# A finer-stepped opening behind dummy matmuls, and two weight subtractions given to GpSimd at the boundary into latent attention

## The reference, cut to what matters

```python
def dilated_mixer(x, w_in, w_out, cos, sin):
    h = x @ w_in                      # 2048 x 20480, in fp32
    ...
def mla_mixer(x, w_in, ...):
    h = x @ w_in
...
for layer in range(DEPTH):
    ...
    x = layer_norm(DEEPNORM_ALPHA * x + y, ln_g[layer], ln_b[layer])
```

## Time and profile before

| what | value |
|---|---|
| time, median of 3 runs | 2507.94 us (2507.93 to 2508.31) |
| profiled execution, its own time | 2507.58 us |
| its span | 2505.8 us |
| PE, DVE, ACT, POOL busy | 99%, 75%, 49%, 1% |
| PE's waits that the trace names, first 60 us | 10.3 us |
| the same, boundary into MLA (1090 to 1160 us) | 4.4 us |

### The profile page before, as it was taken

How to read it: one execution, slowest core, us unless ns; L and a number is a source line. 1 busy time by engine, 2 the same in 40 slices (tenths; PEclk the granted TensorE clock), 3 DMA queues, 4 the chain that set the end, 5 groups by cost and what they waited for, 6 DMA issues and landing times.

```text
span 2505.8 us, 33399 instructions
## 1 busy us (share of the span) xinstructions
PE 2480.9 (99%) x12591; PEld 2093.0 (84%) x12591; DVE 1889.1 (75%) x3357; ACT 1236.4 (49%) x1825; POOL 17.3 (1%) x37
## 2 busy tenths in 40 slices
PE   8999999999999999999999999999999999999999
PEld 6888888888888888878888869888888898888887
DVE  7888988898888888675555557666986767678865
ACT  4444444444444444445555456553455665444553
POOL 0000000000000000000000000000000000000000
PEclk9999999999999999999999999999999999999999
DMA  8787778777877787655545436444446544444554
GB/s 310 258 296 276 258 264 299 279 260 262 295 268 262 266 295 251 213 183 168 160 156 175 166 105 199 159 135 141 162 156 188 176 155 153 146 139 151 167 169 135
DMA packets 266113, 517.03 MB, mean 206 GB/s; under 512 B 16624, under 2 KB 21072, under 8 KB 265312
## 3 DMA queue, kind: packets, MB, share of 16 engines
q1 hardware_dynamic: 264256, 508.43, 59.5%
q0 software_dynamic: 1696, 6.47, 1.0%
HBM read 512.76 MB, written 2.10 MB: 205 GB/s over the span
## 4 chain that ended last, share of the span: by engine, by line
PE 90%; DVE 7%; issue 2%; ACT 1%; DMA 0%; DVEq 0%; SPq 0%; ACTq 0%
PE proj L585 15%; PE proj L587 15%; PE proj L586 15%; PE proj L1239 8%; PE proj L1241 8%; PE proj L1240 8%; PE scores L715 3%; DVE w_lo L1862 2%; PE proj L1231 1%; PE proj L1233 1%; PE proj L1234 1%; PE proj L625 1%; DVE arena L1987 1%; PE proj L627 1%; PE proj L626 1%
## 5 line engine op out<-in xcount | busy, mean ns | idle before, releaser
L1862 DVE TENSOR_TENSOR w_lo<-w_raw,w_hi 128x1024 fp32r<-128x1024 f32 (+1 forms) x740 | 895.2, 1218 | 288.7 <-ACT w_hi L1280 230.6
L1280 ACT ACTIVATE w_hi<-w_raw 128x1024 fp32r<-128x1024 f32 (+1 forms) x740 | 774.7, 1053 | 622.4 <-PE proj L587 382.4
L585 PE MATMUL proj<-w_hi,xt_lo 128*128 128x512 f32 x1632 | 651.1, 399 | 4.6 <-DVE xt_lo L1877 4.5
L587 PE MATMUL proj<-w_hi,xt_hi 128*128 128x512 f32 x1632 | 637.6, 391 | 0.0
L586 PE MATMUL proj<-w_lo,xt_hi 128*128 128x512 f32 x1632 | 636.3, 390 | 0.0
L1239 PE MATMUL proj<-w_hi,xt_lo 128*128 128x512 f32 x976 | 395.6, 405 | 0.3 <-DVE w_lo L1862 0.3
L1241 PE MATMUL proj<-w_hi,xt_hi 128*128 128x512 f32 x976 | 381.1, 390 | 0.0
L1240 PE MATMUL proj<-w_lo,xt_hi 128*128 128x512 f32 x976 | 380.5, 390 | 0.0
L585 PEld LDWEIGHTS proj<-w_hi,xt_lo 128*128 128x128 f32 x1632 | 307.3, 188 | 66.2 <-DVE xt_lo L1877 6.3
L587 PEld LDWEIGHTS proj<-w_hi,xt_hi 128*128 128x128 f32 x1632 | 306.7, 188 | 65.7
L586 PEld LDWEIGHTS proj<-w_lo,xt_hi 128*128 128x128 f32 x1632 | 307.3, 188 | 60.5
(11 more groups left out here) (405 smaller groups left out, 2753.0 us busy)
## 6 DMA issues: line engine op xcount, KB each, us to landing
w_raw<-in_dsa_w_in_dram SPq DMA_DIRECT2D x159, 1024.0 KB, 7.5
w_raw<-in_w_in_dram SPq DMA_DIRECT2D x120, 1024.0 KB, 5.1
arena<-in_w_ada_dram SPq DMA_DIRECT2D x192, 512.0 KB, 6.1
w_raw<-in_w_out_dram SPq DMA_DIRECT2D x32, 1024.0 KB, 5.1
w_raw<-in_mla_w_in_dram SPq DMA_DIRECT2D x24, 1024.0 KB, 5.1
w_raw<-in_dsa_w_out_dram SPq DMA_DIRECT2D x16, 1024.0 KB, 5.0
w_raw<-in_mla_w_out_dram SPq DMA_DIRECT2D x16, 1024.0 KB, 5.1
w_raw<-in_mla_w_ukv_dram SPq DMA_DIRECT2D x8, 1024.0 KB, 5.4
```

The lines of the kernel that those rows point to most:

```text
L585: mm(o, xt[1][:, k0 + kk, tok], WH[:, c % 2, k, 0:n], start=first, stop=False)
L587: ins = mm(o, xt[0][:, k0 + kk, tok], WH[:, c % 2, k, 0:n], start=False, stop=last)
L1280: A(hi[:, 2 * q:2 * q + 2, 0:n], RAW[:, c % 4, 2 * q:2 * q + 2, 0:n], ACT.Copy).then_inc(hi_made, 1)
L1862: V.tensor_tensor(lo[:, ks, 0:n], RAW[:, c % 4, ks, 0:n], hi[:, ks, 0:n].bitcast(F32), ALU.subtract).then_inc(lo_made, 1)
```

## The change

In the opening:

- The identity comes alone (128 columns of the constants); the rest of them follows later. The first group of x comes in two DMAs of 256 columns, issued by ACT. The first two k-tiles of the weights come in a DMA each.
- DVE's first instruction is now the fill of `ONES`; PE begins with 7 matmuls on it (128 x 128, fp32), whose results nobody reads (`warm_up`).
- Half 0 is worked in steps: `first_half` on PE, `first_his` and `first_part` on ACT, `first_lows` and `first_part_low` on DVE. The hi*hi matmuls of a k-tile come first, then those with the low part of x, then those with the low part of the weights. The number of matmuls of the half, 12, stays.
- Groups 1 and 3 of x are turned into the PSUM banks `SP` and `PV` (called `scores` and `attended`) and so no longer wait for a free `TP`.
- `X_AT` is (1, 3, 5) for groups 1 to 3, before it was (0, 3, 6, 8) for groups 0 to 3. `angles` moves from after half 1 to after half 2, `sines` to after half 4, `tables_of` from after half 6 to after half 8. On ACT the sine moves from after half 3 to after half 5, the silu of c to after half 7.

At the boundary `low_in` for halves 12 and 13 is taken from DVE's list, and POOL makes them (`low_by_pool`).

```diff
-X_AT = (0, 3, 6, 8)
+X_AT = (1, 3, 5)
...
-            sp.dma_start(CST[:, 0:K_MASK], io["constants"][:, 0:K_MASK]).then_inc(ident_loaded, 16)
-            load_x(0)
+            sp.dma_start(IDENT, io["constants"][:, 0:K_INV]).then_inc(ident_loaded, 16)
             first = w[0:CK * P, 0:BW].rearrange("(k p) n -> p k n", p=P)
-            sp.dma_start(RAW[:, 0, 0:2], first[:, 0:2]).then_inc(first_half_loaded, 16)
+            sp.dma_start(RAW[:, 0, 0:1], first[:, 0:1]).then_inc(w_first, 16)
+            sp.dma_start(RAW[:, 0, 1:2], first[:, 1:2]).then_inc(first_half_loaded, 16)
...
+            act.dma_start(X[:, :, 0:256], x[:, :, 0:256]).then_inc(x_first, 16)
+            act.dma_start(X[:, :, 256:512], x[:, :, 256:512]).then_inc(x_loaded[0], 16)
...
+            def warm_up():
+                pe.wait_ge(warm, 1)
+                for _ in range(7):
+                    mm(PV[:, 0:P], ONES[:, :], ONES[:, :], start=True, stop=True)
...
+            def first_half():
+                turn_first(0)
...
+                pe.wait_ge(turn_hi, 1)
+                pe.wait_ge(first_hi, 1)
+                for k in range(2):
+                    if k == 1:
+                        turn_first(1)
+                        pe.wait_ge(hi_made, 1)
+                    for t in range(T):
+                        mm(PJ[0][t][:, :], XTH[:, k, t * P:(t + 1) * P], WH[:, 0, k, :], start=k == 0, stop=False)
+                    if k == 0:
+                        pe.wait_ge(turn_lo, 2 + 1)
+                    for t in range(T):
+                        mm(PJ[0][t][:, :], XTL[:, k, t * P:(t + 1) * P], WH[:, 0, k, :], start=False, stop=False)
...
+            def first_his():
+                act.wait_ge(w_first, 16)
+                A(WH[:, 0, 0, :], RAW[:, 0, 0, :], ACT.Copy).then_inc(first_hi, 1)
+                first_part(0)
+                act.wait_ge(first_half_loaded, 16)
+                A(WH[:, 0, 1, :], RAW[:, 0, 1, :], ACT.Copy).then_inc(hi_made, 1)
+                first_part(1)
...
+            def first_lows():
+                dve.wait_ge(first_hi, 1)
+                V.tensor_tensor(WL[:, 0, 0, :], RAW[:, 0, 0, :], WH[:, 0, 0, :].bitcast(F32), ALU.subtract).then_inc(first_lo, 1)
+                first_part_low(0)
+                dve.wait_ge(hi_made, 1)
+                V.tensor_tensor(WL[:, 0, 1, :], RAW[:, 0, 1, :], WH[:, 0, 1, :].bitcast(F32), ALU.subtract).then_inc(lo_made, 1)
+                first_part_low(1)
...
             norm_take(1)
-            low_in(C_MLA_IN, 12)
             norm_part(1, 0)
-            low_in(C_MLA_IN, 13)
             norm_part(1, 1)
...
+            def low_by_pool(seam, c0):
+                for n, h in enumerate((12, 13)):
+                    c, q = chunk_at(c0, h), h % 2
+                    pool.wait_ge(hi_made, 2 * c + q + 1)
+                    hi, lo = halves_of(c)
+                    ks = slice(2 * q, 2 * q + 2)
+                    nc.gpsimd.tensor_tensor(lo[:, ks, :], RAW[:, c % 4, ks, :], hi[:, ks, :].bitcast(F32), ALU.subtract)\
+                        .then_inc(pool_low, 1)
+                    pool.wait_ge(pool_low, 2 * seam + n + 1)
+                    pool.wait_ge(lo_made, 8 + 2 * c + q)
+                    pool.sem_inc(lo_made, 1)
```

More of the change, by code:

```diff
@@ L694, in narrow_turned, with turn_first @@
                 ins.then_inc(half_used, 2)
+            def warm_up():
+                pe.wait_ge(warm, 1)
+                for _ in range(7):
+                    mm(PV[:, 0:P], ONES[:, :], ONES[:, :], start=True, stop=True)
+            def turn_first(part):
+                if part == 0:
+                    pe.wait_ge(ident_loaded, 16)
+                pe.wait_ge((x_first, x_loaded[0])[part], 16)
+                for t in range(T):
+                    for kt in (2 * part, 2 * part + 1):
+                        ins = nc.tensor.transpose(TP[t][:, kt * P:(kt + 1) * P], X[:, t, kt * P:(kt + 1) * P], IDENT)
+                ins.then_inc(turned, 1)
+            def first_half():
+                turn_first(0)
+                pe.wait_ge(dve_evacuated, 1)
+                pe.wait_ge(act_evacuated, 1)
+                pe.wait_ge(turn_hi, 1)
[8 more added lines that the diff above has]
+                        pe.wait_ge(turn_lo, 2 + 1)
+                    for t in range(T):
+                        mm(PJ[0][t][:, :], XTL[:, k, t * P:(t + 1) * P], WH[:, 0, k, :], start=False, stop=False)
+                    if k == 0:
+                        pe.wait_ge(first_lo, 1)
+                    else:
+                        pe.wait_ge(lo_made, 8 + 1)
+                    for t in range(T):
+                        ins = mm(PJ[0][t][:, :], XTH[:, k, t * P:(t + 1) * P], WL[:, 0, k, :], start=False, stop=False)
+                ins.then_inc(half_used, 1)
             def turn_in(g):
@@ L761, in columns @@
                 ins.then_inc(ada_columned, 1)
-            pe.wait_ge(ident_loaded, 16)
-            turn_in(0)
+            warm_up()
             def windows():
@@ L1267, in round_half @@
             def round_half(c, q, n=BW):
-                if c == 0 and q == 0:
-                    act.wait_ge(first_half_loaded, 16)
-                elif c == 0 or q == 0:
+                if c == 0 or q == 0:
                     act.wait_ge(raw_loaded[c % 4], 16 * (c // 4) + 16)
@@ L1855, in _ @@
                 dve.sem_inc(s, n)
+            V.memset(ONES[:, :], 1.0).then_inc(warm, 1)
             def low_half(c, q, n=BW):
@@ L1877, in lo_in, with first_part_low @@
                     V.tensor_tensor(XTL[:, 4 * g:4 * g + 4, t * P:(t + 1) * P],
-                                    TP[t][:, :].rearrange("p (k s) -> p k s", k=4), hi.bitcast(F32),
+                                    bank_of(g, t)[:, :].rearrange("p (k s) -> p k s", k=4), hi.bitcast(F32),
                                     ALU.subtract).then_inc(turn_lo, 1)
+            def first_part_low(part):
+                dve.wait_ge(turn_hi, part + 1)
+                ks = slice(2 * part, 2 * part + 2)
+                for t in range(T):
+                    cols = slice(t * P, (t + 1) * P)
+                    own(V.tensor_tensor(XTL[:, ks, cols], TP[t][:, part * 256:part * 256 + 256].rearrange("p (k s) -> p k s", k=2),
+                                        XTH[:, ks, cols].bitcast(F32), ALU.subtract))
+                own.sync()
+                dve.sem_inc(turn_lo, 1)
+            def first_lows():
[5 more added lines that the diff above has]
+                first_part_low(1)
             def block_done(c):
@@ L1917, in angles @@
                 dve.wait_ge(pos_loaded, 32)
-                dve.wait_ge(ident_loaded, 16)
+                dve.wait_ge(inv_loaded, 16)
                 own(V.tensor_copy(small[:, 4:8], small[:, 0:4].bitcast(I32)))
-                own(V.memset(ONES[:, :], 1.0))
                 own.sync()
```

61 lines of the change are left out of this document (43 added, 18 removed).

## The result

The changed kernel takes 2504.43 us (median of 20 runs, 2504.07 to 2505.87), the kernel before on the same chip 2508.16 (20 runs, 2507.71 to 2511.12). The ratio is 0.9986, interval 0.9979 to 0.9992: 3.7 us, or 0.14%, so within the bound of 0.2%. The forecast was 2504.2. The 20 runs fall in two groups, 14 from 2504.07 to 2504.84 and 6 from 2505.40 to 2505.87; the profiled one is of the first.

A forecast was written before the change was run, and what follows sets the result against it. PE was taken as the bound, busy 2480.9 of 2505.8 us. Gains of 2.5 (opening) and 1.15 (boundary) make 3.65, from 2507.58 to 2503.9; with 0.36 for the median, 2504.2, range 2502.0 to 2506.3.

The forecast's parts named there:

- the exclusive port: Boundary: POOL and DVE shut each other out of SBUF for a whole operation; gain 1.15 us; chance 0.45.
- Both terms: The two gains that were added: 2.5 us from the opening and 1.15 us from the boundary.
- my early bound of 5.3: Opening: earliest landing of the first weights, about 5.3 us; 5.8 was taken, the old landing 7.34 being the late bound.
- the alternative: Opening: TensorE's clock rises only about 11 us, leaving 1.5 us of the opening's 2.5.
- half 0 ends 1.9 later, of which the wait for half 1 hides 0.9: Opening: the working for a clock that rises only about 11 us, leaving 1.5 us of gain.
- What is given back: Opening: moved steps cost PE 0.3 us at half 4, 1.15 at half 5, 1.2 at half 6; half 8 at 36.8.
- The cap: Half 22: DVE's smallest lead on PE, 2.6 + 0.25, lets at most 2.85 us of the opening's gain survive; 2.5 taken.
- -1.5 at 4.0: Boundary: the gain becomes -1.5 us if DVE and POOL exclude each other and a POOL operation lasts 4.0 us.
- The free port: Rival at the boundary: POOL runs beside DVE without delay, gain 2.65 us, total time 2502.8; chance 0.28.
- The low clock: Rival in the opening: clock stays low or landings hardly sooner, 2505.3 to 2506.4 us; chance 0.14.
- Landings 0.6 sooner: Rival in the opening: transfers 0.6 us sooner through a second queue, opening 3.4 us, total 2501.9 to 2503.4; chance 0.09.
- The slow side: Rival at the boundary: POOL's subtraction is long; from 10 us an operation, slower by 1 us and more; chance 0.04.

The follow-up runs named there:

- The later sine: The changed kernel with ACT's sine behind half 6's high part and the silu behind half 8's; median 2504.03 us.
- boundary_only: The kernel before with the low parts of halves 12 and 13 on POOL and nothing else; 2507.19 us against 2508.17 for the kernel before.
- pool_later: The changed kernel, with POOL asking for its first subtraction only when DVE has made half 11's low part; median 2504.16 us.
- pool_double: The changed kernel with each of POOL's two subtractions made twice, with the same result; median 2508.96 us.

## Why the prediction held, step by step

**Where the time goes.** The forecast of 2504.2 and its range held, and so did the likeliest case, the exclusive port. But between the two traces the sum was 3.07, not 3.65. Both terms were too large, by 0.46 and by 0.23 (0.1 more came behind the boundary), and that the median still came within 0.2 us of the forecast is in part luck. The forecast is the 2503.93 of the sum and 0.36 for a median above the profiled execution (2504.29, if it isn't rounded down). The profiled execution was the missing 0.58 higher, at 2504.51, and the median was 0.08 below it instead of 0.36 above. The ratio is helped from the other side: the median of before was 0.58 above its profiled execution, and its long runs count in that. The difference of 3.73 is 3.07 + 0.58 + 0.08. I had no term for a spread that differs between the kernels.

**The start.** First product 6.75 (forecast 7.15), half 1 at 12.39 (12.7), half 2 at 15.32 (15.7): the first weights' rounding began at 5.28, so they had landed by my early bound of 5.3, not at 5.8. The bound itself doesn't follow from its rate: 0.07 MB less at 0.5 MB in 1.6 us is 0.2 us, which gives 5.6. The order of causes was right down to half 2's low part.

**The clock.** The forecast took the 2.4 GHz level for half 0 and named the alternative, 1.0 lost and 1.5 left of the opening. By the times, 14 of 20 runs of the changed kernel had the 2.4 GHz level and 6 the loss, of 1.3. That most of the 20 were early is luck too, as half of the 64 runs with these dummies are late; a late median would have been about 2505.7, inside the range. The step "half 0 ends 1.9 later, of which the wait for half 1 hides 0.9" was right in kind: without dummies half 0 ends 2.3 later (12.55 against 10.28), and 1.31 of it reaches half 1. The Trainium skill, TensorE: Matmul & The Clock Gate, What's actually happening, says that the array starts throttled and that activity releases it; the kernels with none and with four dummies agree, with 0.43 us a matmul at the start of half 0.

**What is given back.** PE waited 0.90 before half 5 (forecast 1.15), 1.47 before half 6 (1.2) and 0.30 before half 4 (0.3), and half 8 came at 37.02 (36.8). Both longer waits have the releasers that the text named. The later sine shows that half 6's is ACT's.

**The cap.** This is the term that was mis-sized. I had 2.6 of lead at half 22 plus 0.25, because my schedule put DVE's half 11 at 41.8. In the trace it begins at 42.40, 0.36 later than before, and the same 0.36 is there at half 22: the low part is ready at 77.39 against 77.03, not 0.25 sooner. So 2.27 was left, 2.22 reached half 22, and 2.03 the boundary. The schedule had the sine, for PE at half 6, but no line of it has the silu, whose table load and operation delay half 8's high part by 1.5 us and leave DVE idle for 1.06. With sine and silu a step later, DVE's half 22 was ready 1.23 us sooner.

**The boundary.** The mechanism was right: first come, first served, for a whole operation. The price was 2.38 us an operation, not 2.0. The working took the operation's length less 0.5 of slack from the 2.65, which gives 0.77 at 2.38, and 0.92 came: DVE stood for 2.2 us and PE waited 1.29 of that, so the slack was 0.9. The text's -1.5 at 4.0 doesn't follow from that rule, which gives about -0.9. The Trainium skill, SBUF — State Buffer, Who interferes with whom, states the exclusion. The Trainium skill, GPSIMD Engine Reference, Elementwise — side-by-side cycle accounting, gave an estimate of 2.3 us and by it 0.85. The traces agree with both, with 2.35 going to 4.55 and 0.75 to 2.85 us, and POOL at 2.38; for this term the page was the better source than my rows.

**The rivals.** The free port is ruled out by the stretched operations in `boundary_only`, `pool_later` and `pool_double`. The low clock exists, as a share of the runs rather than as the case. Landings 0.6 sooner: the first product came 0.4 sooner than forecast, and nothing of it is left behind the cap. The slow side needs a POOL operation about twice as long, as the doubled kernel shows; POOL's first operation took no more than its 2.38 us and its 0.75 of waiting.

## What to carry to other kernels

Before giving an idle engine a part of a busy one's work, look at what the busy one does in those very microseconds: here the same operation of 2.4 us cost DVE nothing beside steps that read one tensor or PSUM, and 1.9 to 2.2 us beside steps that read two tensors in SBUF. A gain at the start of a long pipeline is worth only the smallest lead of the second engine later on, so put every moved step in the schedule, the small ones too (here a silu of 0.22 us with a table load of 1.28), and carry the idle time that it makes to the place where the lead is smallest. When repeated runs of one kernel fall in two groups, profile until both are caught, and compare group with group: a median of 11 runs moves by 1.3 us with the share of late runs. Here a clock that rose early in half of the executions could be made to do so in all.

## What the runs showed of the hardware

- A POOL subtraction of 1024 columns takes 2.37 to 2.40 us where nothing delays it. Against DVE instructions with two SBUF tensors it is all or nothing: whoever asks first works at full speed and the other stands, up to 2.2 us.
- DVE subtractions that read PSUM and SBUF (0.69 us), statistics (0.70) and the single-tensor steps weren't stretched beside POOL at all.
- The column of the granted clock reads 1.00 in the first microseconds in all of these kernels, also where half 0's matmuls stand 0.42 to 0.43 us apart; there the pace of the matmuls tells the clock and the column doesn't. In the fall at 1118 us the column shows it, as 0.50.
- At the boundary, a wait of 1.90 us and 1.3 us of matmuls were followed by the fall to 1.2 GHz in one profiled execution, and by none in another of another kernel with the same wait: 3.4 us hung on it. In a third kernel the fall came within a wait of 1.35 us, behind one of 1.87 and 0.66 us of transposes, and lasted about 3.4 us.
